# Norm weights and head factors of the sparse branches' q and k: from VectorE to GpSimd in a two-layer hybrid decoder trunk

## The reference, cut to what matters

```python
def rms_norm(x, g, eps=RMS_EPS):
    xf = x.astype(jnp.float32)
    y = xf * lax.rsqrt(jnp.mean(xf * xf, axis=-1, keepdims=True) + eps)
    return (y * g.astype(jnp.float32)).astype(x.dtype)
...
    q_b = rms_norm(qkv_b[:, :, 0], qn_moba).transpose(0, 2, 1, 3)
    k_b = rms_norm(qkv_b[:, :, 1], kn_moba).transpose(0, 2, 1, 3)
...
    q_c = rms_norm(qkv_c[:, :, 0], qn_dsa).transpose(0, 2, 1, 3)
    k_c = rms_norm(qkv_c[:, :, 1], kn_dsa)
```

## Time and profile before

| | |
|---|---|
| median of 3 runs | 991.32 us |
| the profiled execution's own time | 991.47 us |
| its span | 989.3 us |
| TensorE busy (matmul) | 935.7 us, 95% |
| VectorE busy | 694.0 us, 70% |
| ScalarE busy | 482.7 us, 49% |
| GpSimd busy | 24.4 us, 2% |
| mean granted TensorE clock | 0.976 of full speed |

### The profile page before, as it was taken

One profiled execution on the slowest core, in us unless ns is written; L12 is line 12 of the kernel. 1 busy time (PEld: TensorE's weight loads), 2 busy tenths in 40 slices (PEclk: granted clock), 3 DMA queues, 4 the chain that ended last, 5 costly groups with the idle time before them and its releaser, 6 DMA issues.

```text
span 989.3 us, 15954 instructions
## 1 busy us (share of the span) xinstructions
PE 935.7 (95%) x6744; PEld 880.1 (89%) x6744; DVE 694.0 (70%) x1087; ACT 482.7 (49%) x654; POOL 24.4 (2%) x49
## 2 busy tenths in 40 slices
PE   8998989998998999999989998999989899999998
PEld 6787969976987999999978997898779799999998
DVE  4997889787784656666574797988878555656443
ACT  4554776455445433343463468374553454333341
POOL 1010000000000000000000000000000000000000
PEclk8999999999998999999989999999999789999999
DMA  9979633414652776767545795251454434654541
GB/s 361 384 285 373 238 114 132 171 44 171 255 213 86 256 255 216 280 237 281 181 170 183 273 327 187 92 204 45 172 211 173 171 128 171 218 207 172 178 164 43
DMA packets 29593, 198.31 MB, mean 200 GB/s; under 512 B 3282, under 2 KB 3794, under 8 KB 7507
## 3 DMA queue, kind: packets, MB, share of 16 engines
q1 hardware_dynamic: 23474, 155.22, 43.6%
q0 software_dynamic: 5760, 41.95, 11.5%
q10 hardware_dynamic: 288, 0.14, 0.0%
HBM read 196.24 MB, written 1.05 MB: 199 GB/s over the span
## 4 chain that ended last, share of the span: by engine, by line
PE 62%; DVE 24%; ACT 7%; issue 4%; DMA 3%; ACTq 0%; DVEq 0%
PE bank L479 16%; PE bank L481 16%; PE bank L480 16%; DVE w_lo L1174 7%; ACT w_hi L873 2%; DVE front L1181 2%; DVE score L1346 2%; DMA raw<-in_slabs_dram 2%; DVE acc L1437 2%; PE bank L506 1%; PE bank L586 1%; PE bank L585 1%; PE bank L587 1%; DVE score L1364 1%; ACT acc L1083 1%
## 5 line engine op out<-in xcount | busy, mean ns | idle before, releaser
L1174 DVE TENSOR_TENSOR w_lo<-raw,w_hi 128x2048 fp32r<-128x2048 f32 (+2 forms) x146 | 314.6, 2160 | 138.7 <-ACT w_hi L873 137.1
L479 PE MATMUL bank<-h_hi,w_hi 128*128 128x256 f32 x1216 | 350.8, 289 | 12.1 <-DVE w_lo L1174 6.2
L873 ACT ACTIVATE w_hi<-raw 128x2048 fp32r<-128x2048 f32 (+2 forms) x146 | 262.9, 1806 | 175.0 <-PE bank L481 120.9
L481 PE MATMUL bank<-h_hi,w_lo 128*128 128x256 f32 x1216 | 347.2, 286 | 0.0
L480 PE MATMUL bank<-h_lo,w_hi 128*128 128x256 f32 x1216 | 347.2, 285 | 0.0
L479 PEld LDWEIGHTS bank<-h_hi,w_hi 128*128 128x128 f32 x1216 | 236.5, 194 | 16.7 <-issue 14.9
L480 PEld LDWEIGHTS bank<-h_lo,w_hi 128*128 128x128 f32 x1216 | 236.5, 195 | 0.1
L481 PEld LDWEIGHTS bank<-h_hi,w_lo 128*128 128x128 f32 x1216 | 236.4, 194 | 0.0
L479 PE MATMUL bank<-y_hi,w_hi 128*128 128x256 f32 x480 | 135.6, 282 | 2.2 <-DVE w_lo L1174 2.2
L480 PE MATMUL bank<-y_lo,w_hi 128*128 128x256 f32 x480 | 135.1, 282 | 0.0
L481 PE MATMUL bank<-y_hi,w_lo 128*128 128x256 f32 x480 | 135.0, 281 | 0.0
(11 more groups left out here) (171 smaller groups left out, 1151.2 us busy)
## 6 DMA issues: line engine op xcount, KB each, us to landing
raw<-in_slabs_dram SPq DMA_DIRECT2D x124, 1024.0 KB, 5.1
front<-in_ada_dram POOLq DMA_DIRECT2D x31, 1024.0 KB, 5.7
acc<-in_ada_dram POOLq DMA_DIRECT2D x9, 1024.0 KB, 5.7
raw<-in_slabs_dram SPq DMA_DIRECT2D x16, 552.0 KB, 4.9
front<-in_ada_dram SPq DMA_DIRECT2D x5, 1024.0 KB, 11.4
raw<-in_slabs_dram SPq DMA_DIRECT2D x6, 768.0 KB, 6.7
proj<-in_ada_dram SPq DMA_DIRECT2D x2, 1024.0 KB, 9.1
x_t<-in_x_dram SPq DMA_DIRECT2D x2, 512.0 KB, 5.3
```

What stands on the lines that cost most here:

```text
L479: nc.tensor.matmul(b_out, st_hi, mv_hi, start=start, stop=False, skip_group_check=True)
L481: return nc.tensor.matmul(b_out, st_lo, mv_hi, start=False, stop=stop, skip_group_check=True)
L873: nc.scalar.activation(w_hi[:, n % RING, 0:w], raw[:, n % RING, 0:w], ACT.Copy).then_inc(hi_ready.sem, 1)
L1174: nc.vector.tensor_tensor(w_lo[:, n % RING, 0:w], raw[:, n % RING, 0:w], w_hi[:, n % RING, 0:w], ALU.subtract).then_inc(lo_ready.sem, 1)
```

## The change

`pair_norm` of VectorE becomes `pair_factors` (reciprocal and head factors, which then raise a new semaphore `pf_done`), at the same two places of VectorE's program. The three large multiplications of each branch go to GpSimd's program, behind its ten loads of the layer and ahead of the two that wait for scored heads. There branch C comes first: a wait for the layer's norm weights and for both `psq_done` (so that the squares of both branches are read before q and k are overwritten), two multiplications by the norm weights, a wait for `pf_done` once, the multiplication by the factors (`pn_done`); then the same for B with a wait for `pf_done` twice. TensorE, ScalarE and SyncE keep their programs.

```diff
--- before.py
+++ after.py
@@ -334,6 +334,7 @@
         psq_done = event("psq_done", 2)
         pss_done = event("pss_done", 2)
         pstd_done = event("pstd_done", 2)
+        pf_done = event("pf_done", 2)
         pn_done = event("pn_done", 2)
         pair_tp = event("pair_tp", 2)
         pq_out = event("pq_out", 2)
@@ -370,6 +371,7 @@
         glu_hi_done = event("glu_hi_done", FG)
         glu_lo_done = event("glu_lo_done", FG)
         dve_chain = event("dve_chain", 0)
+        pool_chain = event("pool_chain", 0)
         act_chain = event("act_chain", 0)
         warm = event("warm", 0)
         out_stored = event("out_stored", 0)
@@ -436,11 +438,30 @@
                 pool.wait_ge(ada_used.sem, KT + (before[-1] + 1 if before else 0))
                 pool.dma_start(ada_raw[place], ada[l, tile]).then_inc(ada_in[place].sem, 16)
 
+            link = Chain(pool, pool_chain)
+
+            def pair_norm(l, kind, base, ss, g0):
+
+                if kind == 0:
+                    pool.wait_ge(gains_in.sem, gains_in.at(l, 16))
+
+                    pool.wait_ge(psq_done.sem, psq_done.at(l, 2))
+                v = proj[:, :, base:base + 512].rearrange("p t (g d) -> p t g d", d=HD)
+                for m in range(2):
+                    gm = gains[:, g0 + HD * m:g0 + HD * (m + 1)].unsqueeze(1).unsqueeze(1).to_broadcast([P, TT, 4, HD])
+                    ins = nc.gpsimd.tensor_tensor(v[:, :, 4 * m:4 * m + 4, :], v[:, :, 4 * m:4 * m + 4, :], gm, ALU.mult)
+                link(ins)
+                pool.wait_ge(pf_done.sem, pf_done.at(l, kind + 1))
+                nc.gpsimd.tensor_tensor(v, v, ss.rearrange("p (t g) -> p t g", t=TT).unsqueeze(3)
+                                        .to_broadcast([P, TT, 8, HD]), ALU.mult).then_inc(pn_done.sem, 1)
+
             n = 0
             for l in range(DEPTH):
                 for _ in range(10):
                     load_ada(n)
                     n += 1
+                pair_norm(l, 0, C_C, ss16, 2 * A_QK + 2 * HD)
+                pair_norm(l, 1, C_B, ss16b, 2 * A_QK)
 
                 pool.wait_ge(scored.sem, scored.at(l, B_HEADS + A_HEADS))
                 for _ in range(2):
@@ -1316,22 +1337,13 @@
                 ada_next()
                 pair_sums(1, ss16b)
 
-                def pair_norm(kind, base, ss, g0, fac):
+                def pair_factors(kind, ss, fac):
 
                     dve.wait_ge(pstd_done.sem, pstd_done.at(l, kind + 1))
-                    v = proj[:, :, base:base + 512].rearrange("p t (g d) -> p t g d", d=HD)
                     link(nc.vector.reciprocal(ss, ss))
-                    link(nc.vector.tensor_tensor(ss, ss, konst[:, fac:fac + 16], ALU.mult))
-                    for m in range(2):
-                        gm = gains[:, g0 + HD * m:g0 + HD * (m + 1)].unsqueeze(1).unsqueeze(1)\
-                            .to_broadcast([P, TT, 4, HD])
-                        ins = nc.vector.tensor_tensor(v[:, :, 4 * m:4 * m + 4, :], v[:, :, 4 * m:4 * m + 4, :], gm,
-                                                      ALU.mult)
-                    link(ins)
-                    nc.vector.tensor_tensor(v, v, ss.rearrange("p (t g) -> p t g", t=TT).unsqueeze(3)
-                                            .to_broadcast([P, TT, 8, HD]), ALU.mult).then_inc(pn_done.sem, 1)
-
-                pair_norm(0, C_C, ss16, 2 * A_QK + 2 * HD, K_FAC + 16)
+                    nc.vector.tensor_tensor(ss, ss, konst[:, fac:fac + 16], ALU.mult).then_inc(pf_done.sem, 1)
+
+                pair_factors(0, ss16, K_FAC + 16)
                 lo(l, S_UKV)
 
                 for h in range(IDX_HEADS):
@@ -1348,7 +1360,7 @@
                                                                  op1=ALU.add)
                         ins.then_inc(idx_acc.sem, 1)
                     if h == 7:
-                        pair_norm(1, C_B, ss16b, 2 * A_QK, K_FAC)
+                        pair_factors(1, ss16b, K_FAC)
                         lo(l, S_GATE1)
                     if h == 11:
                         lo(l, S_GATE1 + 1)
```

## The result

The changed kernel took 996.6 us (median of 5 runs, 995.33 to 998.46) beside 991.36 us before (5 runs, 991.14 to 992.78): the ratio is 1.0051, 95% interval 1.0036 to 1.0065, slower by about 5 us. The profiled execution took 995.33 us with a span of 993.5 us, 4.2 more than before. Most of what follows therefore stands on lengths of stages inside the traces.

What follows compares the result with a forecast made beforehand. VectorE's sums of B's squares were taken to bind ScalarE's root, the relus and TensorE. From 991.47 us, 2 x 2.06 - 0.2 = +3.9 gave 995.4, with the median 0.15 lower: 995.2 us, range 990.6 to 998.1.

Steps and rivals of the forecast that it cites:

- What bounds the stage: Ahead of C's multiplications VectorE's sums of B's squares bind; their delay moves ScalarE's root, the relus and TensorE as much.
- The disputed term: GpSimd's norm-weight multiplications beside `ada_next`'s halves: 0 if undisturbed, 2.06 us per layer if they take turns.
- The choice between the ends: Whether GpSimd and VectorE reading SBUF don't disturb each other or take whole-instruction turns; turns were taken, chance 0.42.
- Rival (a): No disturbance, or GpSimd's turn only at VectorE's pauses or one-input sums: -0.2 us, 991.1 us; chance 0.35.
- (b): Only one multiplication before the sums, or engines partly slowing each other: 1.03 us per layer, 993.2 us; chance 0.13.
- The price of the factors: GpSimd's 128x1024 multiplication by the factors, taken as two memset-like streams: 1.88 us.
- What VectorE loses is worth nothing: 2.5 us leave VectorE per branch; worth nothing for C, 0.1 us per layer for B behind head 7.
- Rival (c): The 2.5 us VectorE saves behind head 7 show in full, 986.3 us; chance 0.05.
- Cover of the results: Slack before TensorE asks for GpSimd's results at 148.37 us and after: 6.8 us for B, 20 us for C.
- Rival (d): GpSimd far slower, TensorE waiting for `pn_done` from 8.7 us per 128x1024 on; 993.7 us at 10 us; chance 0.05.
- The sum: Turns of 2 x 2.06 us less 0.2 us saved behind head 7: +3.9 us, 995.2 us as median.
- the likeliest case: GpSimd and VectorE take turns at `ada_next`'s halves: 995.2 us, reaching from 993.2 to 998.1 us; chance 0.42.

Runs made afterwards that it cites:

- e3: The kernel before with `pair_sums(1)` ahead of the second `ada_next` in place of behind it; median 991.16 us, ratio to before 0.9984 (0.9964 to 1.0003).
- e1: The changed kernel, but GpSimd's first multiplication waits for the sums of B's squares rather than the squares; median 992.12 us, ratio to before 0.9988.
- e2: The kernel before plus two GpSimd multiplications of 128x512 per layer on an unused part of `front`, VectorE keeping its work; 995.62 us, ratio 1.0029.
- e6: The kernel before plus five GpSimd memsets of 128x1024 per layer, from the end of B's squares on; median 991.82 us, ratio 0.9990.
- e7: The changed kernel with norm weights kept on VectorE, GpSimd multiplying only by the factors, once per branch; median 994.58 us, ratio to before 1.0011.
- the second comparison: The changed kernel, unaltered, timed again beside the kernel before on another chip; medians 996.04 and 993.28 us, ratio 1.0012 (0.9989 to 1.0036).
- e4: The changed kernel with `pair_sums(1)` ahead of the second `ada_next`; median 991.97 us, ratio to before 0.9989 (0.9973 to 1.0005).

## Why the prediction was right

- **What bounds the stage.** Right for the stage. VectorE's sums, ScalarE's root, the relus and TensorE are one chain; 2.06 us put in at its head came out as 2.06 us at ScalarE's and TensorE's waits, and e3 took 2.4 us out by the same door.
- **The disputed term.** Taken at 2 x 1.03 = 2.06 us per layer; the halves grew by 2 x 1.03. That both figures agree to the hundredth is luck: 1.03 was two memset streams, and GpSimd's multiplication takes 1.26 us when it is alone (2.52 for two in e1), of which it holds VectorE up for 1.03. The choice between the ends, turns or none, was the step that carried the forecast; e1, e2 and e6 show that it was right, each by its own edit. Rival (a), no disturbance, had 0.35 and is refuted; of (b), one turn only or each engine slowing the other in part, the traces show two turns, and e7 whole ones.
- **The price of the factors.** 1.88 us forecast, 1.90 us measured where nothing disturbs it. The estimate from the Trainium skill, GPSIMD Engine Reference, section "Performance versus the Vector engine", 1.12 and 2.25 us, is on either side of 1.26 and 1.90; the measurement decides.
- **What VectorE loses is worth nothing.** Right, and even more so than written: the 0.1 us per layer behind head 7 was 0.03 us (from the relu of head 8 to the transposes 4.48 us, 4.51 before), since other waits moved first. Rival (c) falls: VectorE idled 3.67 us there. This holds for the clock as it was; layer 1 of e1 shows 0.6 us for it.
- **Cover of the results.** Right. B's factors, 142.75 to 146.57, came behind `lo(S_GATE1)` as I had them, and their 3.82 us hold that wait; the relu of head 8 came at 147.94 and TensorE's transposes at 152.42. One turn I had not counted: B's norm weights met `lo(S_UKV)` and the first `TENSOR_SCALAR` and ended at 134.78 rather than at about 130 (132.9 with the root's delay); the `TENSOR_SCALAR` took 0.89 in place of 0.55 us, and the cover took that up. Rival (d) falls. In e7, where the cover was thinner, a turn cost 0.27 us, and in layer 1 of e1, where the kv projection was early, the sums of heads 8 to 11 took 4.47 us: the bound that I had kept for this was real.
- **The sum.** +3.9 us forecast, +5.2 us measured by the medians, 5.7 in the stage. What was missing is the lower granted clock behind the wait, 1.2 and 0.5 us; the prediction had no term for it, though the clock was below full there before as well (0.83). The measured time lies within the range, and within the likeliest case's own. How close the number came is in part luck: the stage lost more than forecast (5.7 and 5.1 us), and the whole time of the second comparison less (2.8 us).

## What to carry to other kernels

A move from VectorE to GpSimd can pay only where VectorE is last, and it costs where a turn of GpSimd falls into a stretch in which VectorE is last. So place GpSimd's work by what VectorE runs beside it: idle time or sums like those here, not instructions with two input tensors, and not `TENSOR_SCALAR` either. Let it wait for a semaphore that keeps it off the critical stretch; here one later wait took the loss of the stage away. Before moving work off an engine, look at the chain for work that merely stands in front of what the others wait for: swapping two steps on VectorE shortened this stage by 2.4 us per layer, of which some 1.6 lasted in the traces, against nothing for moving 5 us of multiplications away. And where the whole time of a kernel wanders by several microseconds, cut the traces at fixed instructions and compare the pieces.

## What the runs showed of the hardware that I had not expected

- GpSimd's multiplication of 128x512 by a repeated row takes 1.26 us and of 128x1024 1.90 us, so from the one to the other its time rises by half. A blocked one is recorded as longer: 3.82 us for the same 128x1024 beside `lo(S_GATE1)`.
- With VectorE's queue never empty, GpSimd still got its turn: two multiplications passed between `lo(S_UQ + 2)` and the sums, one against each half of `ada_next`. Neither engine was shut out, and VectorE lost 1.03 of GpSimd's 1.26 us per turn.
- Sums with one input (1.21 us beside a GpSimd multiplication in e4, 1.21 alone) and five GpSimd memsets (halves of 1.28 us in e6) disturb nothing. `TENSOR_SCALAR` of 128x128 and 128x256 with one input tensor is held up: 2.81 us for the two in e4 and 1.59 in e1, 0.55 alone.
- At nearly the same wait TensorE did the same products in 8.49, 10.18 and 11.44 us, at granted clocks of 1.00, 0.83 and 0.73.
- The instruction that stands new in GpSimd's order ahead of its first multiplication took 37 ns at 104.7 us, far from anything that waits.
